# One core, a two-layer hybrid decoder trunk: keys are scaled first, PSUM banks are split three and four, and the S5 states start one inverse level earlier

## The chip, the cores and the metric

The kernel runs on 1 core of one Trainium2 chip, in one launch. The metric is device time in microseconds (us), from the first to the last instruction of the core and what lies around it. The time before is 1349.58 us, the median of 3 runs (1348.81 to 1350.08). The execution that the profiler recorded took 1352.41 us; its span, from the first to the last recorded instruction, is 1349.9 us.

## The reference, cut to what matters

```python
SEQ, D_MODEL, DEPTH, D_FF = 256, 1024, 2, 2816        # everything is float32
for l in range(DEPTH):
    x = x + 0.5 * swiglu(rms_norm(x, ffn1_norm[l]), ...)
    x = x + hybrid_mixer(rms_norm(x, mix_norm[l]), ...)
    x = x + 0.5 * swiglu(rms_norm(x, ffn2_norm[l]), ...)
return rms_norm(x, final_norm)

# hybrid_mixer: one input projection, four branches, sigmoid gates, one output projection
# A gated DeltaNet: 4 heads of 64, chunks of 64
lower = jnp.where(strict, beta[..., None] * kk * decay, 0.0)
sol = triangular_solve(lower, rhs, left_side=True, lower=True, unit_diagonal=True)
attn = jnp.einsum("bhncd,bhnmd->bhncm", q, k) * decay
# B S5: complex diagonal recurrence, 16 groups x 64 states
x_re, x_im = associative_scan(combine, (a_re, a_im, bu_re, bu_im), axis=1)
# C Griffin RG-LRU: h * gelu(yb)          D RetNet retention, rotary, chunks of 128
gates = jax.nn.sigmoid(gate_logits.reshape(bsz, s, N_BRANCH, D_MODEL))
merged = jnp.sum(gates * jnp.einsum("bsnc,ncd->bsnd", branches, w_branch), axis=2)
return merged @ w_out
```

## The kernel before

Activations lie transposed, 128 features on the partitions and 256 tokens along the free axis. Every float32 product with a weight is made of three TensorE matmuls in fp32r: high weight by high input, high weight by low input, low weight by high input (lines 447, 448 and 449, in `product`). A weight piece is 128 x 1024 numbers. It goes through a fixed pipeline: SyncE starts its DMA into one of three `raw` slots once the piece three before it has its low part; ScalarE casts it to `whi` (line 905) into one of four slots, once TensorE has used the piece four before it; VectorE subtracts, `wlo` = `raw` - `whi` (line 1303), GpSimd doing this for some later pieces. `split_to(n)` and `ahead(unit)` place these casts and subtractions by hand between an engine's other work: `ahead("g1")` makes all pieces up to two behind the last one of unit `g1`.

Each engine runs a program in an order written out by hand, and semaphores join them. There are two sequences of units that TensorE writes into PSUM. `MAIN` holds the big products (a unit is two halves of 24 matmuls in one bank), `SIDE` the small ones of the mixer. `Units` gives a unit the bank (its number in the sequence) modulo (the number of banks), and TensorE, before it writes a unit, waits until ScalarE or VectorE has taken the unit that last had this bank (`main_bank`, `side_bank`, lines 451 and 458). Before the change `MAIN` has banks 0 to 3 and `SIDE` banks 4 to 6; bank 7 collects the S5 output.

The stretch that the change touches lies in each layer's mixer, between the input projections and the merge. TensorE's order there is: `gate(0)`; transposes of k and v (`ktr`, `vtr`, line 665); decay rows spread over a bank (`gb0`, `gb1`, line 673); `gate(1)`; `kk0, bb0, kk1, bb1` (k against k, line 686, and beta, line 673); `gate(2)`; `qk0, qk1` (line 686); `gate(3)`; then six levels that build the inverse of the triangular matrix. Here `gate(i)` is the big product `g{i}` of 48 matmuls. In a level `lv`, for each half `hp` of the heads: `t{hp}_{lv}` (16 small matmuls, line 733), half of the big product `g{4+lv}` (24 matmuls), and from level 1 on `xy{hp}_{lv}` (32 small matmuls, line 744). In the levels 0 to 3 follow two S5 input products, `pq{2lv}` and `pq{2lv+1}` (`s5_in`, lines 704 and 705), and in the levels 1 to 4 two S5 output products (`s5_out`, lines 713 and 714).

VectorE has for each S5 state pair tile `s` a `s5_state(s)`: four elementwise operations and two scans (lines 1689 to 1698); they read `pq{s}`, and its bank is free at the first scan's end. GpSimd then rotates back (`s5_back`, lines 1240 to 1244) into `tmpE` for even `s` and `tmpF` for odd `s`, which `s5_out` reads. GpSimd also masks the triangular matrix for each level (`level_blocks`, line 1229), first after VectorE's `attn` (line 1681); `y_first` (line 1268) lets level 0 begin.

Ahead of all this VectorE scales q and k (line 1624, `k_normed`, which lets TensorE begin `ktr`), finishes the Griffin branch (lines 1628, 1629), makes the low parts of `g1.0` and `g1.1`, multiplies `qdec` (1632), and only then scales the transposed keys out of the bank of `ktr` (`kbe`, `kdec`, lines 1645, 1646) and the values (1651). After the low parts of `g2.0` and `g2.1` come the decay differences (1667), and with ScalarE's exponentials (1141) the products of lines 1672, 1674 and 1677.

In the merge, TensorE makes for each of 8 row tiles two units `mg{m}a` and `mg{m}b` of 12 matmuls each; VectorE takes each with one operation (line 1841).

Of the kernel before, what the change touches and what calls it, by code (L numbers as in the profile page):

```python
# [31 lines left out]
ALU = mybir.AluOpType  # L32
# [104 lines left out]
for _name, _n, _ in STREAM:  # L137
# [5 lines left out]
           if _n.startswith("mg") or _n in [f"g{_k}.1" for _k in range(11, 16)] + ["wo0.0", "wo1.0"]]  # L143
# [9 lines left out]
         ("ktr", "dve"), ("vtr", "dve")]  # L153
        + [(n, "dve") for n in ("gb0", "gb1", "kk0", "bb0", "kk1", "bb1", "qk0", "qk1")]
        + [u for lv in range(LEVELS) for u in
           ([u for hp in range(2) for u in [(f"t{hp}_{lv}", "act")] + [(f"{n}{hp}_{lv}", "dve") for n in LEVEL_UNITS[lv]]]
            + [(f"pq{s}", "dve") for s in ([2 * lv, 2 * lv + 1] if lv < 4 else [])]
            + ([("rotq", "dve"), ("rotk", "dve")] if lv == 4 else []))]
# [49 lines left out]
def trunk(nc, weights, params, consts, positions, x_in, y_out):  # L208
    ctx = ExitStack()
    with ctx:  # L210
# [80 lines left out]
        psum = [ctx.enter_context(nc.psum_tensor(f"bank{i}", [P, 512], F32)) for i in range(8)]  # L291
        main = Units(MAIN, psum[0:4])
        side = Units(SIDE, psum[4:7])
        ybank = psum[7]
# [141 lines left out]
        def tensor_layer(pe):  # L436
# [212 lines left out]
            def gate(i):  # L649
                pair(f"g{i}")  # L650
# [44 lines left out]
            over_all("bb1", 32, 1)  # L695
            gate(2)
            against_k("qk0", 0, 0)
            against_k("qk1", 0, 1)
            gate(3)

            def s5_in(s):
                ps = side_bank(f"pq{s}")
                r, c = slice(32 * (s % 4), 32 * (s % 4) + 32), (s // 4) * P
                mm(ps[:, 0:SEQ], par_("sbr", c, c + P)[r], su[r, s // 4, :], start=True, stop=True)
                mm(ps[:, SEQ:512], par_("sbi", c, c + P)[r], su[r, s // 4, :], start=True, stop=True).then_inc(S("side"), 1)

            def s5_out(s):
# [8 lines left out]

            pe.wait_ge(S("main_act"), main.taken("su"))
            for lv in range(LEVELS):
                for hp in range(2):
# [18 lines left out]
                    for n in LEVEL_UNITS[lv]:  # L738
# [6 lines left out]
                        last.then_inc(S("side"), 1)  # L745
                if lv < 4:
                    s5_in(2 * lv)
                    s5_in(2 * lv + 1)
                if 0 < lv < 5:
# [138 lines left out]
        def scalar_layer(act):  # L888
# [246 lines left out]
            gate(0)  # L1135
            act.wait_ge(S("griffin"), 1)
            A(brh[:, 2], griffin, ACT.Copy).then_inc(S("branch_high"), 1)
            ahead("g1")
            for hp in range(2):
                act.wait_ge(S("side_dve"), side.taken(f"gb{hp}"))  # L1140
                A(flat(dec)[:, hp, :], flat(dec)[:, hp, :], ACT.Exp).then_inc(S("dec"), 1)
            gate(1)
            gate(2)
            gate(3)
# [143 lines left out]
        def vector_layer(dve):  # L1288
# [17 lines left out]
            def ahead(unit):  # L1306

                split_to(last_piece(unit) + 3)
# [316 lines left out]
            dve.wait_ge(S("k_normed"), 1)  # L1625

            dve.wait_ge(S("gelu_t"), 1)
            link(V.scalar_tensor_tensor(tmpD, tmpD, 1.0, ly, ALU.add, ALU.mult))
            V.scalar_tensor_tensor(griffin, tmpF, 0.5, tmpD, ALU.mult, ALU.mult).then_inc(S("griffin"), 1)
            ahead("g0")  # L1630
            dve.wait_ge(S("side_act"), side.taken("eb"))
            V.tensor_tensor(qdec, qkv[:, 0:2, :], egb, ALU.mult).then_inc(S("dve_q"), 1)

# [22 lines left out]

            ahead("g1")
            dve.wait_ge(once["masks"], 4)

            for hp in range(2):  # L1660
                ps = side.bank(f"gb{hp}")
                dve.wait_ge(S("side"), side.ready(f"gb{hp}"))
                for t in range(2):
                    for j in range(2):
                        o = (t * 2 + j) * 64
                        h = 2 * t + hp
                        last = V.tensor_scalar(dec[:, hp, t, j, :], ps[:, o:o + 64], rowT[:, j, h:h + 1], 0.0, ALU.subtract, ALU.min)
                last.then_inc(S("side_dve"), 1)
            tj = lambda m, hp: m[:, hp].rearrange("p t j c -> p (t j) c")
            for hp in range(2):  # L1670
# [6 lines left out]
                V.tensor_tensor(flat(low)[:, hp, :], side.bank(f"bb{hp}")[:, 0:256], flat(low)[:, hp, :], ALU.mult).then_inc(S("side_dve"), 1)  # L1677
            ahead("g2")
            for hp in range(2):
                dve.wait_ge(S("side"), side.ready(f"qk{hp}"))  # L1680
                V.tensor_tensor(flat(attn)[:, hp, :], side.bank(f"qk{hp}")[:, 0:256], flat(dec)[:, hp, :], ALU.mult).then_inc(S("side_dve"), 1)  # L1681

            def s5_state(s):
# [14 lines left out]
                V.tensor_tensor_scan(ss[:, 0, :], mag, tmpA[:, 0, :], 0.0, ALU.mult, ALU.add).then_inc(S("s5s"), 1)  # L1698

            dve.wait_ge(S("tables"), 2)  # L1700
            ahead("g3")
            for lv in range(LEVELS):
                for hp in range(2):
                    split_to(last_piece(f"g{4 + lv}") + 2 + hp)
                    for n in LEVEL_UNITS[lv]:
# [3 lines left out]
                        V.tensor_tensor(mxy[:, hp, c], mxy[:, hp, c], side.bank(unit)[:, c], ALU.subtract).then_inc(S("side_dve"), 1)  # L1709
                if lv < 4:  # L1710
                    s5_state(2 * lv)
                    s5_state(2 * lv + 1)
                if lv == 4:
# [358 lines left out]
```

## Time and profile before

| what | value |
|---|---|
| time, median of 3 (lowest, highest) | 1349.58 us (1348.81, 1350.08) |
| the profiled execution's own time | 1352.41 us |
| its span | 1349.9 us |
| TensorE matmuls busy | 1308.1 us, 97% of the span |
| VectorE busy | 931.2 us, 69% |
| ScalarE busy | 660.2 us, 49% |
| GpSimd busy | 230.4 us, 17% |
| mean granted TensorE clock | 0.988 of full |
| HBM read, DMA engines' share | 217.42 MB, 50.4% |

Busy time is the time in which an engine has an instruction under way; it says nothing on what held the others up. TensorE's matmuls overlap one another, so that a matmul with a duration of 280 ns starts 117 ns behind the one before it. What the kernel can win by order alone is TensorE's idle time, with the time it spends at the lower of its two granted clocks (1.2 instead of 2.4 GHz, shown as 0.50), and time in which small matmuls follow one another that could run side by side.

### The profile page before, as it was taken

The page shows a single profiled execution, that of the slowest core. Times are in us where ns is not written, and L with a number is a line of the kernel's source. Part 1 is how long each engine was busy: PE and PEld are TensorE (multiplying, and loading weights), DVE is VectorE, ACT ScalarE, POOL GpSimd, SP SyncE. Part 2 cuts the span into 40 slices and gives each one's busy share as a digit, 9 for nine tenths or more (in the row PEclk, how much of TensorE's full clock was granted, in tenths as well). Part 3 has the DMA queues.
Part 4 walks back from the last instruction along what each step waited for, and adds up shares of the span by engine and source line. Part 5 has one row for each costly group of instructions (what it writes and reads, how often), then busy time and mean ns, then how long its engine had stood idle before and what let it go on. Part 6 is the DMA issues. An engine that isn't in the chain of part 4 may idle for free. (4 is left out here: it accounts for less than half of the span.)

```text
span 1349.9 us, 27445 instructions
## 1 busy us (share of the span) xinstructions
PE 1308.1 (97%) x11728; PEld 1272.2 (94%) x11728; DVE 931.2 (69%) x1435; ACT 660.2 (49%) x953; POOL 230.4 (17%) x183
## 2 busy tenths in 40 slices
PE   8999999989999999999999999999889999999997
PEld 8999999988788999999999999999877899999997
DVE  5788675875966866666657885567678578566654
ACT  6544647642234464444454455477322355544442
POOL 1000011004733610000100000200157254100000
PEclk9999999989999999999999999999999999999999
DMA  5655664533232555666646556454422335555562
GB/s 200 234 185 188 199 195 127 185 123 126 64 126 74 178 179 196 188 196 221 193 144 201 180 176 214 151 174 148 147 82 78 126 112 192 166 188 187 182 206 97
DMA packets 61465, 220.24 MB, mean 163 GB/s; under 512 B 6944, under 2 KB 7200, under 8 KB 60960
## 3 DMA queue, kind: packets, MB, share of 16 engines
q1 hardware_dynamic: 61344, 218.50, 50.4%
q8 instruction: 92, 1.51, 0.5%
q14 instruction: 29, 0.24, 0.1%
HBM read 217.42 MB, written 1.05 MB: 162 GB/s over the span
## 5 line engine op out<-in xcount | busy, mean ns | idle before, releaser
L447 PE MATMUL bank<-xh,whi 128*128 128x256 f32 x2256 | 642.4, 285 | 8.8 <-DVE wlo L1303 7.0
L448 PE MATMUL bank<-xl,whi 128*128 128x256 f32 x2256 | 633.9, 281 | 0.0
L449 PE MATMUL bank<-xh,wlo 128*128 128x256 f32 x2256 | 633.3, 281 | 0.0
L1303 DVE TENSOR_TENSOR wlo<-raw,whi 128x1024 fp32r<-128x1024 f32 (+1 forms) x384 | 469.2, 1244 | 228.9 <-ACT whi L905 227.2
L905 ACT ACTIVATE whi<-raw 128x1024 fp32r<-128x1024 f32 (+1 forms) x414 | 419.6, 1035 | 175.1 <-DMA raw<-weights 91.1
L447 PEld LDWEIGHTS bank<-xh,whi 128*128 128x128 f32 x2256 | 428.3, 190 | 16.2 <-issue 8.0
L448 PEld LDWEIGHTS bank<-xl,whi 128*128 128x128 f32 x2256 | 428.5, 190 | 0.2
L449 PEld LDWEIGHTS bank<-xh,wlo 128*128 128x128 f32 x2256 | 428.1, 190 | 0.0
L447 PE MATMUL bank<-hh,whi 128*128 128x256 f32 x704 | 196.9, 280 | 0.0
L449 PE MATMUL bank<-hh,wlo 128*128 128x256 f32 x704 | 196.8, 280 | 0.0
L448 PE MATMUL bank<-hl,whi 128*128 128x256 f32 x704 | 196.3, 279 | 0.0
L1251 POOL TENSOR_TENSOR flat<-flat 128x256 f32<-128x256 f32 x36 | 35.4, 982 | 745.0 <-ACT flat L931 744.0
L986 ACT ACTIVATE tmpB<-tmpB 128x256 f32<-128x256 f32 x88 | 36.6, 417 | 224.0 <-DVE tmpB L1351 224.0
L448 PEld LDWEIGHTS bank<-hl,whi 128*128 128x128 f32 x704 | 132.3, 188 | 0.0
L447 PEld LDWEIGHTS bank<-hh,whi 128*128 128x128 f32 x704 | 132.3, 188 | 0.0
L449 PEld LDWEIGHTS bank<-hh,wlo 128*128 128x128 f32 x704 | 132.3, 188 | 0.0
L1210 POOL TENSOR_TENSOR wlo<-raw,whi 128x1024 fp32r<-128x1024 f32 x30 | 73.8, 2464 | 86.0 <-ACT whi L905 86.0
L1351 DVE TENSOR_TENSOR tmpB<-bank,invb 128x256 f32<-128x256 f32 x88 | 37.2, 423 | 61.0 <-PE bank L449 59.9
L1130 ACT ACTIVATE wide<-bank 128x512 f32<-128x512 f32 x32 | 19.1, 597 | 82.2 <-PE bank L449 82.2
L1148 ACT ACTIVATE big<-bank 128x256 f32<-128x256 f32 x24 | 9.2, 385 | 84.1 <-PE bank L733 84.0
L1229 POOL TENSOR_TENSOR big<-big,cst 128x256 f32<-128x256 f32 x24 | 16.8, 722 | 189.0 <-DVE big L1681 189.0
L980 ACT ACTIVATE hh<-tmpC 128x256 fp32r<-128x256 f32 x88 | 36.9, 419 | 1.9 <-DVE tmpC L1343 1.9
(366 smaller groups left out, 1444.9 us busy)
## 6 DMA issues: line engine op xcount, KB each, us to landing
raw<-weights SPq DMA_DIRECT2D x350, 512.0 KB, 4.1
raw<-weights SPq DMA_DIRECT2D x64, 448.0 KB, 4.0
cst<-consts SPq DMA_DIRECT2D x1, 1088.0 KB, 8.2
par<-params SPq DMA_DIRECT2D x1, 1072.5 KB, 9.2
par<-params SPq DMA_DIRECT2D x1, 1060.5 KB, 8.3
x<-x_in SPq DMA_DIRECT2D x2, 512.0 KB, 7.4
y_out<-ret SPq DMA_DIRECT2D x4, 256.0 KB, 2.3
ropec<-positions SPq DMA_DIRECT2D x1, 128.0 KB, 8.4
```

Source lines behind the costliest of these rows:

```text
L447: mm(out, w[0], a[0], start=start, stop=False)
L448: mm(out, w[0], a[1], start=False, stop=False)
L449: return mm(out, w[1], a[0], start=False, stop=stop)
L905: A(slot(whi, i), slot(raw, i), ACT.Copy).then_inc(once["high"], 1)
L980: A(hh[:, m, :], tmpC[:, m % 2, :], ACT.Copy).then_inc(S("hh"), 1)
L986: A(tmpB[:, m % 2, :], tmpB[:, m % 2, :], ACT.Silu).then_inc(S(f"silu{f}"), 1)
L1130: A(gates[:, 2 * i:2 * i + 2, :], halves(main.bank(f"g{i}")[:]), ACT.Tanh, scale=0.5).then_inc(S("main_act"), 1)
L1210: tt(slot(wlo, i), slot(raw, i), r32(slot(whi, i)), ALU.subtract).then_inc(S("low_pool"), 1)
L1229: tt(lowc[:, hp].rearrange("p t j c -> p (t j) c"), low[:, hp].rearrange("p t j c -> p (t j) c"), over(lev[:, lv, 0:64], 4), ALU.mult).the ...
L1251: tt(squared[:, 0, :], squared[:, 0, :], squared[:, k, :], ALU.add).then_inc(S("sq_step" if k < KD - 2 else "sq_added"), 1)
L1303: V.tensor_tensor(slot(wlo, i), slot(raw, i), r32(slot(whi, i)), ALU.subtract).then_inc(S("low_dve"), 1)
L1351: V.tensor_tensor(tmpB[:, m % 2, :], main.bank(f"gu{f}_{m}")[:, 0:SEQ], invb, ALU.mult).then_inc(S("gated"), 1)
```

## The change

It has five parts. Banks: `MAIN` gets three banks (0 to 2), `SIDE` four (3 to 6). VectorE's order behind `k_normed`: the low part of `g1.0`, the keys and values, the low part of `g1.1`, the decay differences, and only then the Griffin branch and `qdec`. ScalarE's cast of the Griffin branch moves behind `gate(1)`'s evacuation. TensorE's `pq0` and `pq1` move from the end of level 0 to between `bb1` and `gate(2)`; the later pairs each move one level forward. VectorE's `s5_state(0)` moves ahead of the two `attn` products, `s5_state(1)` ahead of level 0, and the later pairs one level forward. `s5_out` and GpSimd's program keep their order.

```diff
-        + [(n, "dve") for n in ("gb0", "gb1", "kk0", "bb0", "kk1", "bb1", "qk0", "qk1")]
+        + [(n, "dve") for n in ("gb0", "gb1", "kk0", "bb0", "kk1", "bb1", "pq0", "pq1", "qk0", "qk1")]
...
-            + [(f"pq{s}", "dve") for s in ([2 * lv, 2 * lv + 1] if lv < 4 else [])]
+            + [(f"pq{s}", "dve") for s in ([2 * lv + 2, 2 * lv + 3] if lv < 3 else [])]
...
-        main = Units(MAIN, psum[0:4])
-        side = Units(SIDE, psum[4:7])
+        main = Units(MAIN, psum[0:3])
+        side = Units(SIDE, psum[3:7])
...
             over_all("bb1", 32, 1)
-            gate(2)
-            against_k("qk0", 0, 0)
-            against_k("qk1", 0, 1)
-            gate(3)
...
+            pe.wait_ge(S("main_act"), main.taken("su"))
+            s5_in(0)
+            s5_in(1)
+            gate(2)
+            against_k("qk0", 0, 0)
+            against_k("qk1", 0, 1)
+            gate(3)
...
-                if lv < 4:
-                    s5_in(2 * lv)
-                    s5_in(2 * lv + 1)
+                if lv < 3:
+                    s5_in(2 * lv + 2)
+                    s5_in(2 * lv + 3)
...
             gate(0)
-            act.wait_ge(S("griffin"), 1)
-            A(brh[:, 2], griffin, ACT.Copy).then_inc(S("branch_high"), 1)
             ahead("g1")
...
             gate(1)
+            act.wait_ge(S("griffin"), 1)
+            A(brh[:, 2], griffin, ACT.Copy).then_inc(S("branch_high"), 1)
...
             dve.wait_ge(S("k_normed"), 1)
-
-            dve.wait_ge(S("gelu_t"), 1)
-            link(V.scalar_tensor_tensor(tmpD, tmpD, 1.0, ly, ALU.add, ALU.mult))
-            V.scalar_tensor_tensor(griffin, tmpF, 0.5, tmpD, ALU.mult, ALU.mult).then_inc(S("griffin"), 1)
-            ahead("g0")
-            dve.wait_ge(S("side_act"), side.taken("eb"))
-            V.tensor_tensor(qdec, qkv[:, 0:2, :], egb, ALU.mult).then_inc(S("dve_q"), 1)
+            split_to(piece_at("g1.0") + 1)
...
-            ahead("g1")
+            split_to(piece_at("g1.1") + 1)
             dve.wait_ge(once["masks"], 4)
...
                 last.then_inc(S("side_dve"), 1)
+            dve.wait_ge(S("gelu_t"), 1)
+            link(V.scalar_tensor_tensor(tmpD, tmpD, 1.0, ly, ALU.add, ALU.mult))
+            V.scalar_tensor_tensor(griffin, tmpF, 0.5, tmpD, ALU.mult, ALU.mult).then_inc(S("griffin"), 1)
+            dve.wait_ge(S("side_act"), side.taken("eb"))
+            V.tensor_tensor(qdec, qkv[:, 0:2, :], egb, ALU.mult).then_inc(S("dve_q"), 1)
+            ahead("g1")
...
-            ahead("g2")
-            for hp in range(2):
-                dve.wait_ge(S("side"), side.ready(f"qk{hp}"))
-                V.tensor_tensor(flat(attn)[:, hp, :], side.bank(f"qk{hp}")[:, 0:256], flat(dec)[:, hp, :], ALU.mult).then_inc(S("side_dve"), 1)
...
+            ahead("g2")
             dve.wait_ge(S("tables"), 2)
+            s5_state(0)
+            for hp in range(2):
+                dve.wait_ge(S("side"), side.ready(f"qk{hp}"))
+                V.tensor_tensor(flat(attn)[:, hp, :], side.bank(f"qk{hp}")[:, 0:256], flat(dec)[:, hp, :], ALU.mult).then_inc(S("side_dve"), 1)
+
             ahead("g3")
+            s5_state(1)
...
-                if lv < 4:
-                    s5_state(2 * lv)
-                    s5_state(2 * lv + 1)
+                if lv < 3:
+                    s5_state(2 * lv + 2)
+                    s5_state(2 * lv + 3)
```

## Rows read from the trace of the kernel before

**Rows 1.** Waits of PE, whole span: us in total, times, longest us.

```profile
PE bank L673 <- DVE qkvp L1646: 8.0, 2, 4.0
PE bank L733 <- DVE tmpD L1697: 7.2, 4, 2.3
...
PE bank L713 <- POOL tmpF L1244: 3.1, 6, 1.2
```

**Rows 2.** Windows: busy us by engine, granted clock, DMA share, GB/s.

```profile
954.80:958.10 3.30, 3.30 (x18) 3.24 (x16) 3.30 (x9) 1.12 (x2) 0.00 (x0) 0.50 0.59 206
```

**Rows 3.** PE timeline, layer 1, gates 1 and 2: start, us, what, idle before.

```profile
954.26 0.67 PE L673 MATMUL bank<-rows,cst 32*64 32x128 f32 x8 [3.98 <-DVE qkvp L1646]
954.86 0.58 PE L447 MATMUL bank<-xh,whi 128*128 128x256 f32 x1
...
962.16 0.68 PE L686 MATMUL bank<-qkv 64*64 64x64 f32 x16
...
964.54 0.39 PE L447 MATMUL bank<-xh,whi 128*128 128x256 f32 x1
...
970.35 0.97 PE L686 MATMUL bank<-qkv 64*64 64x64 f32 x32
```

**Rows 4.** PE timeline, layer 0, gate 1.

```profile
291.05 0.58 PE L447 MATMUL bank<-xh,whi 128*128 128x256 f32 x1
...
299.09 0.68 PE L686 MATMUL bank<-qkv 64*64 64x64 f32 x16
```

**Rows 5.** DVE timeline, layer 1, the same stretch as Rows 3.

```profile
947.87 0.69 DVE L1624 SCALAR_TENSOR_TENSOR qkv<-qkv,big 128x512 f32<-128x512 f32 x1
...
949.92 2.36 DVE L1303 TENSOR_TENSOR wlo<-raw,whi 128x1024 fp32r<-128x1024 f32 x2
...
952.79 0.42 DVE L1645 TENSOR_TENSOR qkvp<-bank,rowT 128x256 f32<-128x256 f32 x1
...
962.96 0.42 DVE L1674 TENSOR_TENSOR big<-bank,big 128x256 f32<-128x256 f32 x1 [3.95 <-PE bank L686]
```

**Rows 6.** ACT timeline, layer 1: the cast of the second piece of gate 2.

```profile
954.70 1.06 ACT L905 ACTIVATE whi<-raw 128x1024 fp32r<-128x1024 f32 x1 [3.09 <-DMA raw<-weights]
```

**Rows 7.** PE timeline, layer 1, levels 1 and 2 of the inverse.

```profile
992.44 1.12 PE L733 MATMUL bank<-big 64*64 64x64 f32 x16 [2.30 <-DVE tmpD L1697]
993.49 0.58 PE L447 MATMUL bank<-xh,whi 128*128 128x256 f32 x1
...
997.50 1.15 PE L744 MATMUL bank<-big 64*64 64x64 f32 x32
998.58 0.71 PE L704 MATMUL bank<-su,par 32*128 32x256 f32 x4
...
999.64 0.40 PE L713 MATMUL bank<-tmpE,par 128*32 128x256 f32 x1
...
1000.64 0.68 PE L733 MATMUL bank<-big 64*64 64x64 f32 x16
```

**Rows 8.** PE timeline, layer 1, the S5 outputs of level 2.

```profile
1012.46 0.62 PE L713 MATMUL bank<-tmpE,par 128*32 128x256 f32 x2
...
1014.65 0.68 PE L733 MATMUL bank<-big 64*64 64x64 f32 x16
```

**Rows 9.** DVE timeline, layer 1, one pair of states and one level's subtractions.

```profile
999.74 0.69 DVE L1689 TENSOR_TENSOR tmpA<-bank,wide 128x512 f32<-128x512 f32 x1 [0.36 <-PE bank L705]
...
1007.17 1.69 DVE L1303 TENSOR_TENSOR wlo<-raw,whi 128x1024 fp32r<-128x1024 f32 x1
...
1011.51 0.69 DVE L1709 TENSOR_TENSOR big<-big,bank 128x512 f32<-128x512 f32 x1 [0.42 <-PE bank L744]
```

**Rows 10.** POOL timeline, layer 1, beside the DVE row at 1007.17.

```profile
1007.91 2.10 POOL L1240 TENSOR_TENSOR tmpF<-tmpD,wide 128x512 f32<-128x512 f32 x1
```

**Rows 11.** DVE timeline, the merge of layer 1: `mg3a` is taken.

```profile
1116.49 0.69 DVE L1841 SCALAR_TENSOR_TENSOR tmpC<-wide,bank 128x512 f32<-128x512 f32 x1
```

**Rows 12.** PE timeline, the merge of layer 1: the first matmul of `mg4b`.

```profile
1118.34 0.28 PE L447 MATMUL bank<-brh,whi 128*128 128x256 f32 x1
```

More of the change, by code:

```diff
@@ L714, in s5_out @@
                 mm(o, par_("sci", s * 32, s * 32 + 32), xs[:, 1, :], start=False, stop=True, tile_position=(0, q)).then_inc(S("s5y"), 1)
-            pe.wait_ge(S("main_act"), main.taken("su"))
             for lv in range(LEVELS):
```

## The prediction

> **What bounds the kernel now.** I read the page first: TensorE is busy in 97% of the span, so order alone can win only its idle time, time at its lower clock, and small matmuls that could overlap. Next the waits of PE [rows 1]. Three of them belong to the stretch that is changed: 8.0 us in two waits of `gb1` (line 673) for VectorE, 7.2 us in four waits of the levels' `t1` (line 733) for the S5 scans, 3.1 us in six waits of `s5_out` (line 713) for GpSimd. The windows show the second price: the 3.3 us from 954.8, right behind the 4 us wait, had the granted clock 0.50, so 1.2 GHz [rows 2]. Then the timelines of each engine, layer 1 for most of it; layer 0 repeats them within 0.1 us but for the clock.
>
> **Part 1, `gb1` and gate 1.** With three side banks `gb1` has the bank of `ktr`, which VectorE frees only with line 1646, behind Griffin, two low parts and `qdec`; PE idles 3.98 us [rows 3]. With four banks `gb0` and `gb1` get the banks of `rowt` and `eb`, which ScalarE took long before. That wait goes wholly: 4.0 us a layer. Gate 1 then loses its slow clock. Gate 2 takes 5.81 us (964.54 to 970.35), gate 1 took 7.30 (954.86 to 962.16) in layer 1 [rows 3] and 8.04 (291.05 to 299.09) in layer 0 [rows 4]: 1.5 and 2.2 us. What is late next? Gate 1 needs the low parts of `g1.0` and `g1.1`. VectorE leaves `k_normed` at 948.56 [rows 5]; `g1.0` (2.36/2 = 1.2 us) is ready at 949.8, PE starts gate 1 at 950.9 (gb1 now starts at 954.26 - 3.98 = 950.28, and takes 0.6). The six key and value products take about 2.1 us and `g1.1` 1.2 more: 953.1, while PE gets to it at 953.8. Covered by 0.7 us; that is why keys first costs nothing. Part 1: 5.5 us in layer 1, 6.2 in layer 0.
>
> **Part 2, `pq0` and `pq1` ahead of gate 2.** They add no work, since they leave level 0, but they add a wait: their banks are those of `kk0` and `bb0`, which VectorE must have taken. Behind them on PE stands gate 2, so everything waits. VectorE does the same instructions as before between `k_normed` and the product with `kk0`, in another order; before, it was through with them at 962.96 - 3.95 = 959.0 [rows 5]. So `kk0` is taken at 959.5, `bb0` some 0.6 later. PE ends gate 1 at 950.9 + 5.8 = 956.7 and the four small units (962.16 to 964.54, 2.4 us [rows 3]) at 959.1. `pq0` waits 0.4 us, and since `pq1` starts 0.6 behind it, the pair no longer runs as one: it takes 1.06 us together (998.58 to 999.64 [rows 7]), here some 1.5. Cost: 1.0 us a layer. Lower end 0 (VectorE's order saves nothing, PE's may be slower); upper end 3 us: the cast of `g2.1` waited 3.09 us for its DMA [rows 6], which starts when `g1.0`'s low part is made; that is 1.3 us earlier now, but VectorE reaches `g2.1` only at about 957.8, so I take the cast as covered.
>
> **Part 3, S5 one level earlier, and its banks.** Before, `t1_1` and `t1_2` wait for the bank of the second state of the pair just issued: 7.2/2 = 3.6 us a layer [rows 1]. `t1_1` and the half product behind it then take 992.44 to 997.50 = 5.06 us at the slow clock [rows 7], against 0.7 + 5.81/2 = 3.6: another 1.45 us. With four banks `t1` waits for the first state of the pair, `xy1` for the second. Count from the start of level 1, when both of `pq2`, `pq3` have just been written: a pair of states takes VectorE 7.4 us (999.74 to 1007.17 [rows 9]), its banks are free at 3.1 and 6.9 us; PE asks for them at 4.8 and at 8.4 us. Both waits go.
> A level with a pair on PE took 1000.64 to 1014.65 = 14.0 us [rows 7, 8]; less its wait of 1.3 and the 1.2 of part 4 it is 11.5. VectorE's is 7.4 + 4.5 (two low parts, two subtractions; 1007.17 to 1011.51 less 0.42 idle plus 0.6 [rows 9]) = 11.9. So VectorE becomes the slower one in levels 1 and 2, but only there: levels 3 and 4 have no states any more. Where it matters first is `pq7`, whose bank is that of `xy0_2`: VectorE frees it 11.9 + 7.4 + 2.3 = 21.6 us from the start of level 1, PE asks at 21.4. Next `t0_4`: 33.5 against 33.5. I take 0.3 us a layer off; bounds 0 and 2.5 (below, rival 1).
> `s5_state(0)` now stands ahead of `attn`, on which GpSimd's masks and `t0_0` hang. VectorE is at 959.0 plus 2.3 for the rest of `kk` and `bb` (962.96 to their end) plus 2.4 for `g3`'s low parts = 963.7, plus half a pair, 3.7 = 967.4. PE starts gate 2 at 959.1 + 1.0 + 1.06 = 961.1 (964.54 before), ends it at 966.9, and has `qk0` at 967.4: neither waits long for the other, `attn` stands to PE's gate 3 as before, and it costs nothing. `s5_state(1)` follows `attn` (0.8) and `g4`'s low parts (2.4 to 3.4), so that its bank is free near 974.5; `t1_0` wants it at 966.9 + 0.9 + 5.8 + 3.6 = 977.2. Covered.
>
> **Part 4, `s5_out`.** The state of a pair is now made one level ahead, and GpSimd has both ready long before `s5_out`. In level 1 both were ready before too: the two products ran side by side, in 999.64 to 1000.64 = 1.00 us [rows 7]. In level 2, with the second one late, the same eight matmuls took 1012.46 to 1014.65 = 2.19 [rows 8]. Levels 3 and 4 look like level 2, the last one with a wait longer by 1.0 (the longest of the six is 1.2; the four others share 0.7 [rows 1]). Gain: 3 x 1.19 + 1.0 = 4.6 us a layer. Bounds: 1.5 (the waits alone, the pairs staying serial) and 4.6.
> The Trainium skill, TensorEngine Tiling (Array Packing), Key Properties, says that different tiles work in parallel; these products use different groups of 32 columns, and the trace agrees (1.00 against 2.19). By that rule the term is 4.6, without it 1.5.
>
> **Part 5, three main banks.** A big unit now waits for the taking of the one three before it. The narrowest place is the merge: `mg3a` is taken at 1117.18 [rows 11], `mg4b` starts at 1118.34 [rows 12], 1.2 us to spare, and the tiles beside it have the same; in the gates and feed-forward parts over 2 us are left, since a unit lasts 5.8 us there instead of 1.4. Cost nothing. Moving ScalarE's Griffin copy costs nothing: it idles there for 3 us [rows 6].
>
> **Sum.** Layer 1: 5.5 - 1.0 + 3.6 + 1.45 - 0.3 + 4.6 = 13.8 us. Layer 0: 14.5. Together 28.3. The profiled execution took 1352.4 us: 1324.1. It lay 2.8 us above the median of the runs, so on the median's scale 1349.6 - 28.3 = 1321.3; I say 1321. Behind the levels all engines work relative to PE, so that the gain is kept; the wait at line 788 and the one for `g14`'s low part stay.
>
> **Rivals.**
> 1. *VectorE becomes the bound of the levels.* For: 11.9 against 11.5 us, no reserve at `pq7` and `t0_4`. GpSimd now works beside more low parts: one costs 1.69 us with GpSimd at work [rows 9, 10], 1.2 without [rows 5]; three or four more in levels 0 to 2 at 0.5 each. Against: it has 1.5 us lead at the first bank. Price 1.5 to 2.5 us a layer: 1325 to 1327. Chance 0.25. The Trainium skill, SBUF — State Buffer, Who interferes with whom, says that a VectorE instruction with two SBUF inputs contends with a GpSimd one that reads SBUF, and the rows agree (1.69 against 1.2).
> 2. *The wait moves to `pq0`.* If VectorE is late with `kk0` by 2 us more, or if the short wait among short matmuls brings the slow clock once more (1.5 us, as in part 1), each layer loses 1.5 to 3.5: 1324 to 1328. Against: waits of 1.2 us at line 713 were followed by no slow stretch. Chance 0.15.
> 3. *The `s5_out` pairs stay serial* although both are ready: 3 us a layer less, 1327. Chance 0.08.
> 4. *Slower: three main banks bind in the merge.* TensorE makes a tile's two units in 2.8 us, VectorE takes them between additions. Had `mg(m)a` been taken over 1.2 us later, each tile waits; to undo 28 us it needs another 1.8 us in each of 16 tiles, so VectorE 3 us later per tile. From there the time is over 1350, some 1354 at 3.3. The rows speak against it, since VectorE's order there is unchanged. Chance 0.04.
> 5. *Nothing comes of it*: the gaps reappear elsewhere, 1347 to 1352. Chance 0.03.
>
> **Chances and range.** The forecast (1317 to 1324) has 0.45. Rivals 1 to 3 lie within 1324 to 1330, alone or by twos up to 1334. The range is 1316 to 1333: the low end if part 2 costs nothing (2 us) and part 3 nothing (0.6), with 2 us for the spread of one execution's times against the median. A change under 0.2% (2.7 us) can't be told from none. Faster 0.94, same 0.02, slower 0.04.
>
> **What would show it.** In the profile after: no wait at line 673; gate 1 in 5.8 us at clock 1.00; a wait of 0.3 to 1 us at line 704 ahead of gate 2; no wait over 0.5 us at line 733; the outputs of levels 1 to 4 in 1.0 us each, without GpSimd as releaser; PE busy near 98 to 99% of the span. I am wrong if waits of over 1 us for VectorE stand at `pq7`, `xy1` or `t0` of levels 2 to 4 (rival 1), if a slow stretch follows `pq1` (rival 2), or if line 447 waits for a bank in the merge (rival 4).

## The result: 0.6% faster, less than a third of the forecast

The changed kernel takes 1342.36 us (median of 9 runs, 1337.94 to 1345.74), the kernel before, measured beside it, 1350.08 (9 runs, 1348.1 to 1352.17): ratio 0.994, interval 0.9925 to 0.9954. The forecast was 1321 with 1316 to 1333: the direction held, the size and the range did not. Some 8 us were gained instead of 28.3.

First the waits of PE in the kernel after, in the columns of [rows 1]: us in total, times, longest.

```profile
PE bank L447 <- DVE wlo L1305: 5.6, 8, 1.2
PE bank L735 <- POOL big L1270: 4.7, 2, 2.4
...
PE bank L790 <- DVE big L1756: 2.6, 2, 1.3
PE bank L746 <- DVE tmpD L1694: 2.4, 3, 0.9
...
PE bank L699 <- DVE big L1676: 1.2, 2, 0.6
PE bank L735 <- issue: 0.9, 2, 0.5
PE bank L699 <- DVE big L1713: 0.7, 2, 0.4
```

The three waits of [rows 1] are gone, as forecast: none at `gb1` (now line 673 without a releaser), none of `t1` for a scan that long, almost none at `s5_out`. In their place stand 4.7 us at line 735 for GpSimd, which no step of the prediction had, the forecast one at `pq0` (line 699, 0.6 us a layer), and small ones inside the levels. In layer 1's stretch PE's idle time fell from 91.60 - 82.26 = 9.34 us (the same window in the kernel before) to 89.20 - 84.10 = 5.10, yet the stretch became only 2.4 us shorter. The windows show why (from, to, length, busy us of PE, PEld, DVE, ACT, POOL, granted clock, DMA share, GB/s):

```profile
941.30:1030.50 89.20, 84.10 (x969) 74.50 (x967) 67.13 (x99) 25.73 (x38) 44.99 (x46) 0.92 0.33 107
951.90:958.50 6.60, 6.42 (x27) 5.68 (x28) 6.36 (x12) 1.06 (x1) 0.00 (x0) 0.50 0.76 242
972.40:975.60 3.20, 3.20 (x17) 3.20 (x16) 1.97 (x1) 0.95 (x2) 3.20 (x4) 0.50 0.03 5
1006.50:1009.70 3.20, 3.20 (x27) 2.74 (x25) 1.92 (x4) 1.33 (x2) 2.56 (x3) 0.50 0.57 181
```

The two slow pieces that layer 1 had before have gone, the one of [rows 2] and the one behind the first `t1` wait [rows 7], together 6.8 us at 1.2 GHz; three have come, together 13.7 us. PE's timeline holds what each stands behind; these rows answer to [rows 3, 7, 8] (start, duration, what, idle before it and its releaser):

```profile
943.24 0.39 PE L447 MATMUL bank<-xh,whi 128*128 128x256 f32 x1
...
949.04 0.68 PE L686 MATMUL bank<-qkv 64*64 64x64 f32 x16
...
950.85 0.65 PE L673 MATMUL bank<-rows,cst 32*64 32x128 f32 x8
...
952.08 1.58 PE L699 MATMUL bank<-su,par 32*128 32x256 f32 x4 [0.57 <-DVE big L1676]
...
954.44 0.58 PE L447 MATMUL bank<-xh,whi 128*128 128x256 f32 x1
...
962.16 0.97 PE L686 MATMUL bank<-qkv 64*64 64x64 f32 x32
...
971.29 0.68 PE L735 MATMUL bank<-cst,big 64*64 64x64 f32 x16 [2.35 <-POOL big L1270]
...
991.47 0.40 PE L716 MATMUL bank<-tmpE,par 128*32 128x256 f32 x1
...
992.47 0.33 PE L735 MATMUL bank<-big 64*64 64x64 f32 x4
...
1002.02 1.15 PE L746 MATMUL bank<-big 64*64 64x64 f32 x32 [0.76 <-DVE tmpD L1694]
...
1004.60 0.69 PE L699 MATMUL bank<-su,par 32*128 32x256 f32 x2 [0.37 <-DVE big L1713]
```

Read it by gates. Gate 1 now takes 949.04 - 943.24 = 5.80 us at full clock. Gate 2, behind the 0.57 us wait of `pq0`, takes 962.16 - 954.44 = 7.72 instead of the 5.81 of [rows 3]: the slow clock moved from gate 1 to gate 2. The wait of 2.35 us at `t0_0`, with the second slow piece behind it, is new, and so is the 0.37 us wait in level 2, behind which the third begins. The outputs of level 1 run side by side, 992.47 - 991.47 = 1.00 us.

To compare kernels I use the stretch from the first key transpose (line 665) to the rotation product (line 758 or 760). The table gives its length in layers 0 and 1, and the sum, each from one profiled execution:

```
                layer 0  layer 1   sum    at 1.2 GHz (layer 0 / 1)
before            93.0     91.7   184.6   10.2 /  6.8
after             88.9     89.3   178.1   10.2 / 13.7
forecast            -        -    156.3
banks_only        85.5     83.9   169.4    3.4 /  0
keys_banks        84.9     84.9   169.8    3.4 /  3.4
count_fix         86.5     86.1   172.6    6.8 / 10.2
fix_outs_mid      85.4     85.0   170.3    3.4 /  3.4
fix_half          84.5     83.2   167.7    6.8 /  3.4
after_half        85.9     86.3   172.2    6.8 /  6.8
fix_half_mid      80.2     80.0   160.2    0   /  0
```

### The profile page after: what moved, and what is told of

Read it like the earlier page. It is cut to its first block and busy times, and to the rows that moved or that the text cites. A ratio compares the mean times of both kernels' runs of the same rounds, so it can differ in the third digit from the quotient of the medians.

```text
span 1340.6 us, 27447 instructions
## 1 busy us (share of the span) xinstructions
PE 1305.6 (97%) x11728; PEld 1270.8 (95%) x11728; DVE 930.6 (69%) x1435; ACT 659.7 (49%) x953; POOL 222.2 (17%) x183
```

## The experiments

All are single core kernels, each timed in 4 to 6 runs beside the kernel before. That one's median moved between 1348.4 and 1351.0 from one occasion to the next, so kernels are compared by their ratios to it; "by the ratios" means the difference of two ratios times 1350. Their theories: **the count** (units are taken in another order than they are listed, and a consumer waits for the wrong one), **the short wait** (the wait of `pq0` brings the slow clock), **the ring** (states moved ahead while their outputs stay where they were run into the reuse of a few buffers, which GpSimd and VectorE take in turn). Edits below are relative to the kernel after unless another is named.

**banks_only**: the kernel before with nothing but the split of the banks.

```
-        main = Units(MAIN, psum[0:4])
-        side = Units(SIDE, psum[4:7])
+        main = Units(MAIN, psum[0:3])
+        side = Units(SIDE, psum[3:7])
```

> The kernel before with nothing changed but the banks: MAIN 0 to 2, SIDE 3 to 6. Theory A (most of what can be had comes from the banks): the 4.0 us wait at gb1 goes in both layers with its slow stretch (1.5 and 2.2 us), 11.7 us; in the levels the banks also free t1, but the S5 outputs then come up against GpSimd, so that less than 3 us a layer is left of the 5 us there. 1334 to 1339 us on the scale where before is 1350. Theory B (three main banks cost something): waits of line 447 for VectorE or ScalarE appear in the merge or the gates, and the gain is under 8 us. My prediction's own account gives 11.7 + 2 x (5.0 - 3.5) = 15 us.

Measured: 1332.97 us (1330.92 to 1335.88), ratio 0.9876 (0.9859 to 0.9894). Two lines of diff beat the whole change. PE's timeline in layer 1, then its waits:

```profile
941.25 0.36 PE L447 MATMUL bank<-xh,whi 128*128 128x256 f32 x1 [0.44 <-DVE wlo L1303]
...
947.01 0.27 PE L686 MATMUL bank<-qkv 64*64 64x64 f32 x2
...
984.26 0.62 PE L713 MATMUL bank<-tmpF,par 128*32 128x256 f32 x2 [2.04 <-POOL tmpF L1244]
```

```profile
PE bank L713 <- POOL tmpF L1244: 8.2, 6, 2.0
PE bank L447 <- DVE wlo L1303: 7.5, 10, 2.1
...
PE bank L788 <- DVE big L1752: 2.6, 2, 1.3
```

Gate 1 in 5.76 us, no `gb1` wait and no `t1` wait: the bank split alone does that. The wait for GpSimd at `s5_out` grows from 3.1 [rows 1] to 8.2 us, since PE arrives earlier. That is what the S5 move had to remove.

**keys_banks**: the kernel after without the S5 move (banks and keys first). TensorE's part; the list of units and VectorE's `s5_state` go back in the same way.

```
-            s5_in(0)
-            s5_in(1)
...
-                if lv < 3:
-                    s5_in(2 * lv + 2)
-                    s5_in(2 * lv + 3)
+                if lv < 4:
+                    s5_in(2 * lv)
+                    s5_in(2 * lv + 1)
```

> The changed kernel with the S5 products and states put back to where they were before: banks and the keys-first order alone. Theory A: within 1.5 us of banks_only, since with four banks nothing waits for the keys. Where the changed kernel is not faster than this one, the S5 move is what gave the gain back: I expect 1334 to 1339, so 3 to 8 us faster than the changed kernel. Rival: the S5 move is worth what I predicted (some 5 us a layer) and the loss lies in part 1; then this kernel is slower than the changed one.

Measured: 1332.64 (1331.25 to 1335.32), ratio 0.9877 (0.986 to 0.9894). The same as banks_only: keys first brings nothing that shows. And it is some 9 us faster than the kernel after by the ratios (0.9877 against 0.994, intervals apart). So the S5 move, as made, is a loss.

**count_fix**: `pq1` listed and written behind `qk1`.

```
-        + [(n, "dve") for n in ("gb0", "gb1", "kk0", "bb0", "kk1", "bb1", "pq0", "pq1", "qk0", "qk1")]
+        + [(n, "dve") for n in ("gb0", "gb1", "kk0", "bb0", "kk1", "bb1", "pq0", "qk0", "qk1", "pq1")]
...
             s5_in(0)
-            s5_in(1)
             gate(2)
             against_k("qk0", 0, 0)
             against_k("qk1", 0, 1)
+            s5_in(1)
             gate(3)
```

> The changed kernel with pq1 written behind qk1 instead of behind pq0, in TensorE's order and in the list of units. VectorE's takings then happen in the listed order (state 0, attn 0, attn 1, state 1), so that GpSimd's mask for the second half of the heads waits for attn 1 and not for state 1 as well. Theory count: the 2.35 us wait of t0_0 (line 735 for POOL) goes in both layers, with the slow stretch that follows it (1.5 us); the pair pq0, pq1 no longer overlaps (+0.5 us). 6 to 7 us faster than the changed kernel: 1335 to 1337. Rival (VectorE is the bound of the levels whatever starts them): the time comes back as longer waits in levels 1 to 3, gain under 2 us.

Measured: 1336.64 (1333.67 to 1339.03), ratio 0.9902 (0.9885 to 0.992), its interval just apart from that of the kernel after. GpSimd's waits in the kernel after, then its timeline in layer 1, show what was at fault:

```profile
POOL tmpE L1242 <- PE bank L717: 25.3, 6, 5.6
...
POOL big L1231 <- DVE tmpD L1694: 10.5, 2, 5.3
```

```profile
963.79 0.65 POOL L1231 TENSOR_TENSOR big<-big,cst 128x256 f32<-128x256 f32 x1 [93.30 <-DVE big L1702]
...
969.70 0.94 POOL L1231 TENSOR_TENSOR big<-big,cst 128x256 f32<-128x256 f32 x1 [5.27 <-DVE tmpD L1694]
970.60 1.24 POOL L1270 TENSOR_TENSOR big<-cst,big 128x256 f32<-128x256 f32 x2
```

Line 1231 masks `low`, one half of the heads at a time, and in level 0 waits for the taking of `qk0` and `qk1`. For the second half GpSimd waits until `side_dve` has reached the number that the list gives `qk1`, which is the fourth of these units; VectorE takes `pq0`, `qk0`, `qk1`, `pq1` in that order, so the fourth taking is the scan of state 1 (line 1694). GpSimd idles 5.27 us, and `t0_0` behind it is 2.35 us late, in both layers. In count_fix, again GpSimd's timeline, both masks are one block:

```profile
961.12 2.22 POOL L1231 TENSOR_TENSOR big<-big,cst 128x256 f32<-128x256 f32 x2 [91.35 <-DVE big L1702]
```

Shown: the wait and the slow piece at 972.4 are gone, 5.1 us by the ratios (0.9940 - 0.9902 of 1350).

**fix_outs_mid**: count_fix with both outputs of a level between its two `xy` products.

```
+                    if hp == 0 and 0 < lv < 5:
+                        s5_out(2 * lv - 2)
+                        s5_out(2 * lv - 1)
...
-                if 0 < lv < 5:
-                    s5_out(2 * lv - 2)
-                    s5_out(2 * lv - 1)
```

> As count_fix, and the two S5 outputs of a level stand in its middle (behind the first half of the heads) instead of at its end. Theory ring: GpSimd's s5_back(s) waits for s5_out(s-2), and VectorE's scan of state s for s5_back(s-2), so that in the changed kernel states 4 to 7 wait in mid-state (2.4 us idle ahead of the scan) and TensorE for their banks, 0.35 + 0.76 + 0.37 us and a slow stretch in level 2 and 0.5 to 1 us in level 3. With the outputs some 4 us earlier these go: 2.5 to 4 us a layer, 5 to 8 us in all against count_fix, about 1329. Rival (VectorE's own work of 11.9 us a level is the bound): the waits stay, under 1.5 us gain.

Measured: 1337.18 (1335.58 to 1337.47), ratio 0.9905 (0.9887 to 0.9922): nothing gained. VectorE's waits for the ring are gone, but the outputs of level 4 pay for it (the second row is the short wait of `pq0`):

```profile
PE bank L716 <- POOL tmpF L1246: 5.4, 6, 1.9
PE bank L699 <- DVE big L1676: 1.3, 2, 0.7
```

State 7 is asked for half a level earlier than GpSimd has it: 1.86 and 1.83 us of wait in the two layers, and each is followed by 3.4 us at 1.2 GHz. In this profile the short wait of `pq0` (0.69 and 0.60 us) was followed by no slow piece in gate 2.

**fix_half**: count_fix with `pq0` between the halves of gate 2.

```
             pe.wait_ge(S("main_act"), main.taken("su"))
+            half("g2", 0)
             s5_in(0)
-            gate(2)
+            half("g2", 1)
```

> As count_fix, but pq0 is written between the two halves of gate 2 and not ahead of it, where VectorE has long taken kk0. Theory clock (the short wait at pq0 among 3 us of small matmuls is what brings the 3.4 or 6.8 us at 1.2 GHz into gate 2): no wait at line 699, no slow stretch in gate 2, mean granted clock above 0.992, and 0.6 + 1.5 to 3 us a layer: 1330 to 1332. Rival (the slow stretches come from elsewhere, for instance from the small matmuls themselves or by chance of phase): the 0.6 us wait goes alone, 1335 to 1336, and the mean clock stays at 0.986 to 0.992.

Measured: 1331.16 (1329.54 to 1336.88), ratio 0.9861 (0.9837 to 0.9886), touching count_fix's interval at its edge. No wait at line 699 for line 1676 is left, nor a slow piece at gate 2. The wait was 0.6 us a layer and the gain is 5.5 us by the ratios, so most of it is clock. Slow pieces behind the 0.36 us waits of `pq7` in level 2 stay in this profile. Since the intervals touch, it takes after_half below, whose interval is apart from its base, to show the short wait's price.

**fix_half_mid**: fix_half with the outputs of states 0 to 5 in the middle of levels 1 to 3, those of 6 and 7 at the end of level 4.

```
+                    if hp == 0 and 0 < lv < 4:
+                        s5_out(2 * lv - 2)
+                        s5_out(2 * lv - 1)
...
-                if 0 < lv < 5:
+                if lv == 4:
```

> As fix_half, with the S5 outputs of the states 0 to 5 in the middle of the levels 1 to 3, those of 6 and 7 still at the end of level 4. Theory ring: the waits of VectorE's scans for GpSimd go, and with them PE's waits for pq4 and pq5 (1.5 us) and the ones of level 3 (0.7 to 1.5 us); the 1.8 us at the outputs of 6 and 7, which fix_outs_mid showed, don't come back. 2 to 3 us a layer under fix_half: 1325 to 1328. Rival (GpSimd's own 11.4 us a level bound everything): the waits only move to line 716, no gain beyond 1.5 us.

Measured: 1324.92 (1323.2 to 1327.12), ratio 0.9809 (0.9793 to 0.9824), 7.0 us under fix_half by the ratios, intervals apart. The whole stretch of layer 1 in its windows, and, on PE, the outputs of level 2 and those of level 4:

```profile
935.10:1015.00 79.90, 79.14 (x969) 69.59 (x967) 69.83 (x99) 25.75 (x38) 52.92 (x47) 1.00 0.37 118
```

```profile
984.72 0.62 PE L717 MATMUL bank<-tmpE,par 128*32 128x256 f32 x2
...
986.09 0.62 PE L717 MATMUL bank<-tmpF,par 128*32 128x256 f32 x2 [0.33 <-POOL tmpF L1250]
...
987.08 0.68 PE L736 MATMUL bank<-big 64*64 64x64 f32 x16
...
1014.04 0.41 PE L717 MATMUL bank<-tmpE,par 128*32 128x256 f32 x1
...
1015.04 0.48 PE L764 MATMUL bank<-ret,cst 128*128 128x256 f32 x1
```

PE is busy 79.14 of 79.90 us at clock 1.00, and the outputs of level 4 take 1.00 us. Those of level 2 are serial, 987.08 - 984.72 = 2.36 us, and those of level 3 take 2.38: in the middle of a level GpSimd has the odd state a third of a microsecond late. In the kernel after it is the other way round, the outputs of level 4 are serial, and the ring is seen in VectorE's waits and timeline (still the kernel after):

```profile
1028.28 0.62 PE L716 MATMUL bank<-tmpE,par 128*32 128x256 f32 x2
1029.54 0.62 PE L716 MATMUL bank<-tmpF,par 128*32 128x256 f32 x2 [0.21 <-POOL tmpF L1246]
1030.52 0.48 PE L760 MATMUL bank<-ret,cst 128*128 128x256 f32 x1
```

```profile
DVE tmpC L1694 <- POOL tmpE L1246: 10.5, 4, 3.1
```

```profile
996.74 0.69 DVE L1694 TENSOR_TENSOR_SCAN tmpC<-small,bank 128x256 f32<-128x256 f32 x1 [2.39 <-POOL tmpE L1246]
```

```profile
992.70 1.29 POOL L1242 TENSOR_TENSOR tmpE<-tmpC,wide 128x512 f32<-128x512 f32 x1 [5.58 <-PE bank L717]
```

GpSimd's `s5_back(s)` (line 1242) writes the buffer that `s5_out(s-2)` reads and waits for it, six times, up to 5.6 us (the first row under count_fix); VectorE's scan of state s needs the buffer that `s5_back(s-2)` reads, and waits 10.5 us in four times. The rows at 992.70 and 996.74 are one such chain: the scan of state 4 waits for the `s5_back` of state 2, which waited for the output of state 0. So the scan of a state can't run further ahead than four states of the outputs. In fix_half_mid VectorE waits for GpSimd nowhere in the stretch.

**odd_late**: keys_banks with the odd state's output half a level later, a rival way to remove the 8.8 us for GpSimd without the S5 move.

```
+                    if hp == 0 and lv > 1:
+                        s5_out(2 * lv - 3)
...
                 if 0 < lv < 5:
                     s5_out(2 * lv - 2)
-                    s5_out(2 * lv - 1)
```

> keys_banks with the output of each odd state half a level later (behind xy0 of the next level); that of the even one stays. In keys_banks every odd output waits for GpSimd: 2.0 + 1.7 + 0.7 us a layer, and a slow stretch follows the first. Theory: GpSimd is late with the odd state only by that much, nothing else hangs on it, and the ring (s5_back(3) needs s5_out(1)) has 4 us to spare: all these waits go, 8.8 us in two layers, with the slow stretch (1.5 us each) 10 to 11: 1322 to 1324. Rival (GpSimd or VectorE bounds the levels at this point): new waits at line 733 or 713 take it back, gain under 3 us.

Measured: 1335.48 (1334.6 to 1337.52), ratio 0.9891 (0.9874 to 0.9907), not told apart from keys_banks. The theory missed that GpSimd takes its work in a written order too:

```profile
PE bank L733 <- POOL big L1230: 7.6, 4, 2.6
```

```profile
978.87 2.25 POOL L1242 TENSOR_TENSOR lxp<-tmpD,sinE 128x512 f32<-128x512 f32 x1
...
982.48 1.23 POOL L1230 TENSOR_TENSOR big<-big,cst 128x256 f32<-128x256 f32 x2
```

The masks of the next level (line 1230) stand behind the `s5_back` of the pair. PE, which no longer spends its time on the odd output, comes to `t0` early and waits for them at line 733, 2.63 and 2.62 us in level 2 of the two layers, with 6.8 us at 1.2 GHz beside each. The wait changed its place.

**after_half**: the kernel after, with only `pq0` and `pq1` moved between the halves of gate 2; count left wrong.

```
+            half("g2", 0)
             s5_in(0)
             s5_in(1)
-            gate(2)
+            half("g2", 1)
```

> The changed kernel with pq0 and pq1 both between the halves of gate 2, nothing else (the count of takings stays as it is). Theory clock: the 0.6 us wait at line 699 and the slow stretch in gate 2 go (1.5 to 3.5 us a layer), the 2.35 us wait of t0_0 stays with its slow stretch: 1336 to 1338 against 1342 of the changed kernel. If the slow stretch is owed to the small matmuls and not to the wait, it stays, and the time is 1341.

Measured: 1335.96 (1334.67 to 1338.29), ratio 0.99 (0.9885 to 0.9914), apart from the kernel after. Windows at both sides of gate 2's second half, and the wait that stays:

```profile
949.20:952.20 3.00, 3.00 (x28) 2.87 (x24) 2.86 (x7) 0.98 (x1) 0.00 (x0) 1.00 0.80 298
953.30:956.30 3.00, 3.00 (x26) 2.86 (x24) 2.86 (x6) 0.00 (x0) 0.00 (x0) 1.00 0.77 240
```

```profile
PE bank L736 <- POOL big L1271: 4.7, 2, 2.4
```

The clock is 1.00 where it was 0.50, and the 4.7 us of the count stand as before. The gain is 5.4 us by the ratios. So the two faults are separate, at some 5 us each.

**after_mid**: the kernel after with only the outputs of fix_half_mid.

> The changed kernel with the outputs of states 0 to 5 in the middle of levels 1 to 3, nothing else. Theory ring: VectorE's idle time ahead of the scans of states 4 and 6 goes, and with it PE's waits for pq4, pq5 and their successors (1.9 us in level 2, 0.5 to 1 in level 3) and the slow stretch that lies there in the changed kernel: 2 to 3.5 us a layer, 1336 to 1338. Rival (without the repair of the count GpSimd is late with state 1 and its first outputs): a new wait at line 716 in the middle of level 1 takes half of it back, 1339 to 1341.

Measured: 1334.78 (1328.23 to 1339.43), ratio 0.9885 (0.9862 to 0.9909), apart from the kernel after; but its runs lie 11 us apart. The fastest had the mean granted clock 0.995, the slowest 0.989. By the ratios the outputs are worth 7 us here too; how much of that is the ring's waits, and how much of it is the clock's own spread, stays open, since its profile is that of its slowest execution, with the slow pieces behind the short and the long wait in both layers.

**no_keys**: fix_half_mid with the old order of VectorE and ScalarE round the keys (Griffin's products and `qdec` ahead of the keys).

> fix_half_mid (1324.9) with VectorE's and ScalarE's old order around the keys: Griffin and qdec first. Theory: with four banks nothing waits for the keys, and between k_normed and kk0 VectorE does the same work in either order, so within 1 us of fix_half_mid, at most 0.6 us a layer slower at g1.0's low part (that wait stands in banks_only): 1325 to 1327. Rival (keys first is what lets the S5 move pay): 1330 or more.

Measured: 1325.85 (1324.17 to 1326.72), ratio 0.9822 (0.9806 to 0.9837), against 0.9809 (0.9793 to 0.9824): not told apart. Its profile shows waits of 0.37 and 0.48 us for `g1.0`'s low part in the two layers, which keys first removes; that is all of its worth that shows, under 1 us.

**values_first**: fix_half_mid, and VectorE does `values(2)` and `state_up(2)` ahead of S5's gate product and `g12`'s pieces.

```
-            V.scalar_tensor_tensor(tmpE, tmpE, 1.0, su, ALU.add, ALU.mult).then_inc(S("s5g"), 1)
-            ahead("g12")
             values(2)
             state_up(2)
+            V.scalar_tensor_tensor(tmpE, tmpE, 1.0, su, ALU.add, ALU.mult).then_inc(S("s5g"), 1)
+            ahead("g12")
```

> fix_half_mid (1324.9) with the one larger wait of PE that is left in its mixer taken out: VectorE takes the values of chunk 2 and adds up the state (lines 1752 and 1745 of the kernel before) ahead of the S5 gate product (which took 2.3 us beside GpSimd, 0.7 otherwise) and the next low parts. Theory: the 1.28 us wait of state_up(2) goes in both layers and with it the slow stretch that mostly follows it in one layer or both (1.5 us each): 1320 to 1323. Rival (what is put behind, the low parts or the gate product, is then late for TensorE): a wait of 1 us or more at line 447 or at the glu product, 1324 to 1326.

Measured: 1319.26 (1317.7 to 1322.56), ratio 0.9783 (0.9766 to 0.9801), the fastest of all and some 21 us faster than the kernel after by the ratios. The wait that all the others have (2.6 us in two, at a line between 788 and 794) is gone:

```profile
PE bank L447 <- DVE wlo L1309: 8.8, 9, 1.9
...
PE bank L717 <- POOL tmpF L1250: 1.7, 4, 0.7
```

The mean granted clock over its profile is 0.999, against 0.987 of the kernel after. Against fix_half_mid its interval overlaps (0.9801 and 0.9793), so what it adds to that one is likely, not proved; against both kernels of the case it is clear.

## Why the prediction was wrong, and where it was right

Account of layer 1: forecast gain 13.8 us, measured 2.4, so 11.4 missed. From the profile after: the `pq` step 2.8 more than forecast, the wait of `t0_0` with its slow piece 3.9, waits inside levels 1 to 3 about 2.0, their slow piece 1.4, the pair `pq6`, `pq7` torn apart 1.1, level 4's outputs serial 1.2. That is 12.4, of which the forecast had 0.3 as the cost of the levels; the overshoot of 0.7 is within what such differences of single rows can carry. Layer 0 missed 10.4 of its 14.5.

Three steps failed. By the runs the first cost 5.1 us, the second 5.4 to 5.5 and the third 7.0 to 7.4, together some 18 of the 20 us that were missed. The direction came out right because of part 1: the banks alone bring 17 us, and the rest of the change took half of that back.

- **Part 3, the start of the levels: `s5_state(0)` ahead of `attn` "costs nothing", and `s5_state(1)` is "covered".** It was judged by when VectorE would have `attn` ready, and that time was about right (GpSimd's first mask starts at 963.79, and in count_fix the second follows at once). It never asked for what number GpSimd waits. The listed order and VectorE's order differ, so the mask of the second half hung on the scan of state 1. Price: 2.35 us of wait a layer, 5.1 us in all by count_fix.
- **Part 2, the size.** The wait of `pq0` was forecast at 0.4 us and is 0.57. The term of 1.0 us a layer was mis-sized, because the clock was not in it: from the end of `bb1` (950.85 + 0.65 = 951.5) to gate 2 it is 2.94 us where the forecast had 0.4 + 1.5 = 1.9, and gate 2 takes 7.72 - 5.81 = 1.9 us more. Over the pair's 1.06 us of work that is 3.8 instead of some 1.0. Rival 2 named just this with chance 0.15 and 1.5 to 3.5 us; fix_half and after_half bear it out. The argument against it, waits of 1.2 us at line 713 without a slow piece, did not carry over. Some 2 us of small products stand ahead of those waits too, so they are no different in that; and banks_only has one and the same wait of 2.04 us at line 713 in level 1 of both layers, with clock 0.50 behind it in layer 0 (331.0 to 334.2) and 1.00 in layer 1 (984.3 to 987.6). That a wait was not followed by the slow clock in one execution says little about the next.
- **Part 3, levels, and part 4: the dearest one.** The count of VectorE's work per level against PE's left out the ring: neither `s5_back(s)` behind `s5_out(s-2)` nor the scan behind `s5_back(s-2)` was in it. By moving states ahead and leaving outputs where they were, the change used up the ring's whole lead. Rival 1 expected waits at these places, but from VectorE's load; the row says that VectorE itself waits for GpSimd, and with the same load on VectorE the waits go once the outputs are moved (fix_half_mid, after_mid). The 0.3 us should have been about 4.5 (2.0 of waits, 1.4 of clock, 1.1 of the torn pair). In part 4 the outputs of levels 1 to 3 do run side by side (1.0 us in levels 1 and 3, 1.19 in level 2, where the clock falls at their end), so three of its four levels went as said. The Trainium skill, TensorEngine Tiling (Array Packing), Key Properties, says that different tiles can work in parallel, and these rows agree. Level 4 takes 1030.52 - 1028.28 = 2.24, which is the missing one.
- **Part 1 was right.** `gb1` waits no more; gate 1 takes 5.80 us for a forecast 5.81; the forecast 5.5 and 6.2 us make up most of what the banks bring, 17 us with the `t1` waits.
- **Keys first at nothing was right** (keys_banks, no_keys).
- **Part 5 was right but for a trace.** No unit of the merge waits for a bank. Right behind it, where TensorE asks for the banks of `wo0` and `wo1`, the kernel after waits 0.23 us in each layer for VectorE's taking of `mg7a` (`PE bank L467 <- DVE tmpC L1845: 0.5, 2, 0.2`), which the kernel before does not. Rival 4 is refuted.
- **The sum itself was nearly reachable.** fix_half_mid, which has all parts without the three faults, brings 24.4 of the 28.3 us in the stretch. The outputs of levels 2 and 3 that it has serial, 1.4 us each in a layer, are more than the 3.9 us that are missing. The gains that the terms named exist; the conditions under which they hold were not checked in the code.

## What to carry to other kernels

When a unit is moved in a list whose place is its semaphore number, write down for every waiter on that semaphore which instruction makes the count, in the consumer's own order; an order that differs from the list is legal and costs only time. When a producer is moved forward, look for the ring behind it and move the reader that frees it too. And change one thing at a time: two lines of this diff, the split of the banks, held twice the gain of the whole, and the S5 move cost some 9 us until it was mended.

## What the runs showed of the hardware

A wait of 0.54 to 0.69 us of PE amid small products was followed by 3.4 to 6.8 us at 1.2 GHz in the profiles of after, count_fix and after_mid, and by none in fix_outs_mid; without the wait no profile had it there. So a short wait can cost several times its length, but not each time. In level 2 of fix_half even the wait of `pq7`, 0.36 us, had 6.8 us at 1.2 GHz behind it in layer 0 and 3.4 in layer 1. The clock's part also shows in the runs of one kernel: after_mid's went from 1328.2 us at mean clock 0.995 to 1339.4 at 0.989. What decides it between two executions stays open.

One low part took 1.69 us with GpSimd at work and 1.2 without [rows 5, 9, 10]. The stretch of fix_half_mid has GpSimd busy for 52.9 of 79.9 us beside VectorE's 69.8 and PE still idles under 0.8 us, so what rival 1 had priced at 1.5 to 2.5 us a layer, VectorE late through this contention, did not come once VectorE did not wait for the ring. It is not free on the other side: in that profile the second product of `s5_back` (line 1247) takes 2.25 us beside a low part and 1.28 without, and it is GpSimd that has the odd states late for the outputs of levels 2 and 3. What this costs, no run isolates.
